# Heads of an mLSTM mixer on one Trainium2 core: row selection by matmul against rows read back by DMA, chunk 0 without its state product, output transposes in another PSUM bank

## What is computed

```python
b = jnp.swapaxes(jnp.cumsum(lfb, axis=1), 1, 2)
inter = b + m[..., None]
Dm = jnp.where(causal, b[..., :, None] - b[..., None, :] + ih[..., None, :], -jnp.inf)
m_t = jnp.maximum(inter, jnp.max(Dm, axis=-1))
w_inter = jnp.exp(inter - m_t)
s = jnp.einsum('blhd,bshd->bhls', qb, kb) * jnp.exp(Dm - m_t[..., None])
num = w_inter[..., None] * jnp.einsum('blhd,bhde->bhle', qb, C) + jnp.einsum('bhls,bshe->bhle', s, vb)
den = w_inter * jnp.einsum('blhd,bhd->bhl', qb, n) + jnp.sum(s, axis=-1)
h = num / jnp.maximum(jnp.abs(den), jnp.exp(-m_t))[..., None]
C_new = a_prev[..., None, None] * C + jnp.einsum('bshd,bshe->bhde', kw, vb)
```

## Time and profile before

| | us |
|---|---|
| median of 3 runs | 2975.05 |
| lowest and highest run | 2974.89, 2980.57 |
| profiled execution, its own time | 2982.64 |
| its span in the trace | 2980.9 |
| PE busy (matmuls) | 2853.4 |
| DVE busy | 1445.9 |
| ACT busy | 861.9 |
| POOL busy | 130.8 |

### The profile page before, as it was taken

How to read it: one execution, slowest core, us unless ns; L and a number is a source line. 1 busy time by engine, 2 the same in 40 slices (tenths; PEclk the granted TensorE clock), 3 DMA queues, 4 the chain that set the end, 5 groups by cost and what they waited for, 6 DMA issues and landing times. The chain is left out here.

```text
span 2980.9 us, 44355 instructions
## 1 busy us (share of the span) xinstructions
PE 2853.4 (96%) x17489; PEld 2738.9 (92%) x17489; DVE 1445.9 (49%) x3014; ACT 861.9 (29%) x1392; POOL 130.8 (4%) x190
## 2 busy tenths in 40 slices
PE   5899999999999898999999999999899999999997
PEld 3799999999999888989989988998799999999996
DVE  4655454455443736246436434634773434444346
ACT  5422222222213422332333233234531111111114
POOL 2100000000003000000000000000200000000002
PEclk7899999999999999999999999999999999999998
DMA  7133223222210114111111211212111111111111
GB/s 231 45 97 99 98 84 98 98 84 89 66 52 7 57 42 126 50 57 55 53 61 39 66 57 50 69 54 64 54 43 43 42 42 42 42 42 42 42 43 60
DMA packets 167523, 192.98 MB, mean 65 GB/s; under 512 B 7760, under 2 KB 157036, under 8 KB 167349
## 3 DMA queue, kind: packets, MB, share of 16 engines
q1 hardware_dynamic: 166962, 191.12, 20.1%
q10 hardware_dynamic: 342, 0.15, 0.0%
q0 software_dynamic: 96, 0.00, 0.0%
HBM read 172.38 MB, written 18.87 MB: 64 GB/s over the span
## 5 line engine op out<-in xcount | busy, mean ns | idle before, releaser
L521 DVE SCALAR_TENSOR_TENSOR xT<-ps,gate_p,xT 128x384 f32<-128x384 f32 (+1 forms) x624 | 347.3, 571 | 110.5 <-PE ps L801 97.4
L907 PE MATMUL ps<-hhi,mw_hi 128*128 128x384 f32 (+1 forms) x1152 | 387.8, 337 | 9.6 <-DVE mw_lo L1690 7.6
L738 DVE TENSOR_TENSOR hf<-st,ps 128x384 f32<-128x384 f32 x132 | 70.2, 532 | 642.6 <-PE ps L822 640.5
L908 PE MATMUL ps<-hlo,mw_hi 128*128 128x384 f32 (+1 forms) x1152 | 379.4, 329 | 0.0
L909 PE MATMUL ps<-hhi,mw_lo 128*128 128x384 f32 (+1 forms) x1152 | 379.0, 329 | 0.0
L820 PE MATMUL ps<-hhi,wa_hi 128*128 128x384 f32 (+1 forms) x1056 | 349.9, 331 | 16.9 <-DVE wa_lo L728 13.9
L821 PE MATMUL ps<-hlo,wa_hi 128*128 128x384 f32 (+1 forms) x1056 | 347.5, 329 | 0.0
L822 PE MATMUL ps<-hhi,wa_lo 128*128 128x384 f32 (+1 forms) x1056 | 347.1, 329 | 0.0
L820 PE MATMUL ps<-hhi,wb_hi 128*128 128x384 f32 (+1 forms) x1056 | 346.2, 328 | 0.3 <-DVE wb_lo L728 0.3
L822 PE MATMUL ps<-hhi,wb_lo 128*128 128x384 f32 (+1 forms) x1056 | 346.0, 328 | 0.0
L821 PE MATMUL ps<-hlo,wb_hi 128*128 128x384 f32 (+1 forms) x1056 | 345.9, 328 | 0.0
(11 more groups left out here) (295 smaller groups left out, 5141.2 us busy)
## 6 DMA issues: line engine op xcount, KB each, us to landing
ada_raw<-in_w_ada SPq DMA_DIRECT2D x36, 1024.0 KB, 5.1
mw_raw<-in_w_in SPq DMA_DIRECT2D x32, 1024.0 KB, 5.9
wa_raw<-in_w_ffn_in SPq DMA_DIRECT2D x22, 1024.0 KB, 5.1
wb_raw<-in_w_ffn_in SPq DMA_DIRECT2D x22, 1024.0 KB, 5.2
wo_raw<-in_w_ffn_out SPq DMA_DIRECT2D x22, 1024.0 KB, 5.0
ada_raw<-in_w_ada_final SPq DMA_DIRECT2D x8, 1024.0 KB, 5.4
cs<-in_state_mlstm_C SPq DMA_DIRECT2D x32, 256.0 KB, 2.7
out_C_sample<-cs SPq DMA_DIRECT2D x32, 256.0 KB, 2.2
```

The lines of the kernel that those rows point to most:

```text
L521: ins = dve.scalar_tensor_tensor(out=xT[:, m, t0:t0 + wp], in0=ps[:, bank, 0:wp], scalar=gate_p[:, m:m + 1], in1=xT[:, m, t0:t0 + wp], op0 ...
L738: dve.tensor_tensor(M["hf"][:, n, 0:w], M["st"][:, n, 0:w], ps[:, up_bank("b", b, i, n), 0:w], ALU.mult).then_inc(C["hidden"].sem, 1)
L907: pe.matmul(out, wh, xh, start=(j == 0), stop=False)
L908: pe.matmul(out, wh, xl, start=False, stop=False)
```

## The change

1. `m_rows` and `a_prev` are written to DRAM by SP in `gates_and_v` (two DMAs, `m_d` and `a_d`). SP reads row h of each back on all 128 partitions (`load_m`: `mb`, 128 x 1088 numbers, and `ap_`, 128 x 16), for head 0 when the block `heads` begins, for the others at the end of the head before, ahead of the store of the prompt state. `sel`, L1934, L2008 and L1848 go. DVE's subtraction reads `mb` in SBUF and no longer waits for the products of stage 0; that wait now stands behind it.
2. Chunk 0 has no state product (L1947, L1597 of that chunk go); DVE copies the score product and the state update from PSUM where it added before; `C` is no longer cleared.
3. The output transposes of stage 2 go to bank 3, columns 256 to 511. They wait for `st_done` of the job after in place of `inter_done`. Key transposes of job p wait for `inter_done` of job p-1, and keys times queries of job p for `h_kept` of job p-2.

The diff, cut:

```diff
@@ gates_and_v, SP
+                    sp.dma_start(m_d[:, :], m_rows[:, :]).then_inc(m_out.sem, 16)
...
+                    sp.wait_ge(*e_done(1))
+                    sp.dma_start(a_d[:, :], a_prev[:, :]).then_inc(m_out.sem, 16)
@@ heads, SP, end of a head, behind the wait for c_upd(h * 8 + 8)
+                        if not last:
+                            sp.wait_ge(*K["e_ready"](h * NJ + NJ))
+                            load_m(h + 1)
...
+                    def load_m(h):
+                        sp.dma_start(mb[:, :], m_d[bass.ds(h, 1), :].broadcast_to([P, T])).then_inc(K["mb_in"].sem, 16)
+                        sp.dma_start(ap_[:, :], a_d[bass.ds(h, 1), :].broadcast_to([P, 16])).then_inc(K["mb_in"].sem, 16)
@@ heads, ACT
-                        if chunk:
-                            act.wait_ge(*K["inter_mm"](h * 8 + c + 1))
+                        if chunk and c:
+                            act.wait_ge(*K["inter_mm"](h * 7 + c))
...
-                            ins = act.activation(q[:, i, t0:t0 + L], ps[:, 4, 128 * i:128 * i + L], ACT.Copy, scale=ng[:, i:i + 1])
+                            ins = act.activation(q[:, i, t0:t0 + L], ps[:, 3, 256 + 128 * i:256 + 128 * i + L], ACT.Copy, scale=ng[:, i:i + 1])
@@ heads, DVE
-                        dve.tensor_copy(sel[:, :], ident[0:H, bass.ds(h, 1)].broadcast_to([H, P])).then_inc(*own.one())
-                        dve.memset(C[:, :, :], 0.0).then_inc(*own.one())
...
-                        dve.wait_ge(*K["s0"](h * NJ + p + 1))
-                        dve.tensor_tensor(ex[0:L, 0:L], mask[:, :], ps[0:L, 3, 128:128 + L], ALU.subtract).then_inc(K["e_ready"].sem, 1)
+                        if p == 0:
+                            dve.wait_ge(*K["mb_in"](h * 32 + 32))
+                        dve.tensor_tensor(ex[0:L, 0:L], mask[:, :], mb[0:L, t0:t0 + L], ALU.subtract).then_inc(K["e_ready"].sem, 1)
                         if p:
                             scaled(h, p - 1)
-                        else:
+                        dve.wait_ge(*K["s0"](h * NJ + p + 1))
+                        if p == 0:
                             state_n(h)
...
-                        dve.tensor_copy(ap_[:, :], ps[:, 3, 0:16]).then_inc(K["ap_kept"].sem, 1)
@@ heads, PE, stage 0
                             elif p == 1:
-                                pe.wait_ge(*K["inter_done"](h * 8 + 1))
+                                pe.wait_ge(*K["kw_done"](h * NJ + 2))
                             else:
-                                pe.wait_ge(*K["h_kept"](h * NJ + p - 1))
+                                pe.wait_ge(*K["inter_done"](h * 7 + p - 1))
...
+                            if p >= 2:
+                                pe.wait_ge(*K["h_kept"](h * NJ + p - 1))
...
-                        ins = pe.matmul(ps[0:L, 3, 128:128 + L], sel[:, 0:L], M["m_rows"][:, t0:t0 + L], start=True, stop=True)
@@ heads, PE, stage 2
-                        if p < 7:
-                            pe.wait_ge(*K["inter_done"](h * 8 + p + 2))
-                        else:
-                            pe.wait_ge(*K["h_kept"](h * NJ + p))
+                        pe.wait_ge(*K["st_done"](h * NJ + min(p + 2, NJ)))
...
-                        pe.matmul(ps[:, 3, 0:16], sel[:, :], M["a_prev"][:, :], start=True, stop=True).then_inc(K["ap_mm"].sem, 1)
```

More of the change, by code:

```diff
@@ L40 @@
 EPS = 1e-6
-HEAD_STEPS = 148
+HEAD_STEPS = 146
 BIG = 1.0e30
@@ L912, in layer, with gates_and_v @@
         w_d = I["w_in"][0].rearrange("(k p) n -> p k n", p=P)
-        def gates_and_v(M, v_at, free, v_raw, norm):
+        def gates_and_v(M, v_at, free, v_raw, norm, m_d, a_d):
             ar.at = free
@@ L1366, in spatial, with heads @@
             return [v_out(16)] + [mix_out[t](16 * (3 if t == 0 else 2)) for t in range(SLOTS)]
-        def heads(M, free, mixed_d, stored):
+        def heads(M, free, mixed_d, stored, m_d, a_d):
             ar.at = free
@@ L1520, in body @@
                             load(h + 1, 1)
+                    def load_m(h):
+                        sp.dma_start(mb[:, :], m_d[bass.ds(h, 1), :].broadcast_to([P, T])).then_inc(K["mb_in"].sem, 16)
+                        sp.dma_start(ap_[:, :], a_d[bass.ds(h, 1), :].broadcast_to([P, 16])).then_inc(K["mb_in"].sem, 16)
                     for done in stored:
                         sp.wait_ge(*done)
+                    load_m(0)
                     with sp.Fori(0, H - 1) as h:
@@ L1781, in stage1 @@
                         dve.wait_ge(*K["s1"](h * NJ + p + 1))
-                        if chunk:
-                            dve.wait_ge(*K["inter_done"](h * 8 + c + 1))
+                        if chunk and c:
+                            dve.wait_ge(*K["inter_done"](h * 7 + c))
                         if p:
@@ L1786, in stage1 @@
                         src = inter if chunk else inter_s
-                        ins = dve.tensor_tensor(num[0:L, :], src[0:L, :], ps[0:L, 5, 0:DH + 1], ALU.add)
+                        if p:
+                            ins = dve.tensor_tensor(num[0:L, :], src[0:L, :], ps[0:L, 5, 0:DH + 1], ALU.add)
+                        else:
+                            ins = dve.tensor_copy(num[0:L, :], ps[0:L, 5, 0:DH + 1])
                         ins.then_inc(K["b5_read"].sem, 1)
@@ L1798, in stage1 @@
                                           ).then_inc(K["var_ready"].sem, 1)
-                        if chunk:
+                        if chunk and c == 0:
+                            dve.tensor_copy(C[:, :, :], ps[:, 6:8, 0:DH + 1]).then_inc(K["c_upd"].sem, 1)
+                        elif chunk:
                             dve.scalar_tensor_tensor(out=C[:, :, :], in0=C[:, :, :], scalar=ap_[:, c:c + 1],
@@ L1932, in stage0 @@
                         for i in range(2):
-                            pe.matmul(ps[0:L, 3, 0:L], kk[:, i, t0:t0 + L], q[:, i, t0:t0 + L], start=(i == 0), stop=(i == 1))
-                        ins = pe.matmul(ps[0:L, 3, 128:128 + L], sel[:, 0:L], M["m_rows"][:, t0:t0 + L], start=True, stop=True)
+                            ins = pe.matmul(ps[0:L, 3, 0:L], kk[:, i, t0:t0 + L], q[:, i, t0:t0 + L], start=(i == 0), stop=(i == 1))
                         if p == 0:
@@ L1943, in stage1 @@
                             pe.wait_ge(*K["kw_done"](h * NJ + c + 2))
-                            if c:
-                                pe.wait_ge(*K["c_upd"](h * 8 + c))
+                        if chunk and c:
+                            pe.wait_ge(*K["c_upd"](h * 8 + c))
                             for i in range(2):
@@ L2131, in layer @@
         mixed_d = nc.dram_tensor("mixed", [D, T], F32, kind="Internal").ap()
+        m_d = nc.dram_tensor("m_rows_out", [H, T], F32, kind="Internal").ap()
+        a_d = nc.dram_tensor("a_prev_rows", [H, 16], F32, kind="Internal").ap()
         head_w_in = [cnt("h_w_in0"), cnt("h_w_in1")]
-        S = gates_and_v(M, after, ar.at, v, Norm(V_MIX, 24, 32, gate=40, factor=1.0))
+        S = gates_and_v(M, after, ar.at, v, Norm(V_MIX, 24, 32, gate=40, factor=1.0), m_d, a_d)
         stored = spatial(M, S, after + NTT * D * 4, v, mixed_d)
-        heads(M, after, mixed_d, stored)
+        heads(M, after, mixed_d, stored, m_d, a_d)
         ffn(I["w_ffn2_in"][0], I["w_ffn2_out"][0], Norm(V_FFN2, 48, 56, gate=64, factor=0.5))
```

16 lines of the change are left out of this document (6 added, 10 removed).

## The result

| | median | runs | ratio, 95% interval |
|---|---|---|---|
| before | 2974.97 us | 2974.28 to 2980.57 | |
| after | 2945.16 us | 2943.91 to 2947.61 | 0.9897 [0.988, 0.9914] |
| after, second time | 2946.22 us | 2943.99 to 2949.89 | 0.9896 [0.9877, 0.9916] |

Before stands here with a fourth run beside the three of the forecast. The change takes 29.8 us off, and 30.1 the second time (2976.34 less 2946.22); 27.9 were forecast, and both times lie in the range.

The account below looks back on a forecast made before the run. The prediction took PE's own matmul stream in the heads as the bound. Its terms, 14.2 + 1.3 + 3.5 + 8.9 = 27.9 us, came off the median 2975.05, giving 2947.1 us; range 2937 to 2957.

Parts of the forecast that it names:

- Term 1: PE's selecting matmuls in the stages (9 jobs by 4 heads): removing them takes 14.2 us off, lower end 9.2.
- The neighbour's price: Rival at the selecting matmuls: each worth its neighbour's 0.27 us, so 9.2 us off there, 2952.2 in all; chance 0.04.
- Term 2: PE's selection of `a_prev`, once a head: removing it takes 1.3 us off, and PE's next wait stays.
- Term 3: Chunk 0's state product on PE: removing it takes 3.5 us off, 0.87 in each of 4 heads.
- Term 4: PE's wait at the output transposes for ACT's read of `inter`: 8.9 us off, ends 0 and 8.9.
- The new wait for term 4: Rival: PE waits at the sample product or key transposes instead, all of Term 4 given back, 2956.0 us; chance 0.10.
- The clock: Rival, PE's clock at stage entry: three falls end, 2937.5 us, chance 0.11; or one comes per head, 2959.9, chance 0.05.
- The slow rival: End of heads 0 to 2: broadcast reads delay the store of `C` by 30 us, time 2981 us; chance 0.02.

Follow-up runs that it names:

- before again: The kernel before, run once more without edits: 2976.95 us, ratio 0.9999 to its other runs.
- selections back: The changed kernel with PE's two selecting products put back, their results not used: 2965.44 us.
- bank 3 alone: The kernel before with only the output transposes moved to bank 3 and their waits changed: 2965.59 us, ratio 0.9956.

## Why the prediction was right

Right: the sign, the bound (PE's own stream in the heads) and every term's place. The sum of 27.9 came within 1.9 and 2.2 us of the 29.8 and 30.1, in part by luck: one term was 3.0 too small, and 1.2 that was not foreseen went back.

- **Term 1, 14.2.** Right: the step is 0.41 us with the selection back. The neighbour's price (9.2) fell: the product over 4 rows took 0.41 us here, its neighbour over 128 took 0.27. The changeover between unlike products is not the whole of it: in the trace of before the selection's two instructions start at 1250.14 and 1250.35, 0.21 apart, and its neighbour's with as many columns 0.11 apart (1249.60, 1249.71). The rule that I weighed, of the Trainium skill (TensorE: Matmul & The Clock Gate, "Why this matters for your kernels"), says of 32 rows that they take the time of 128; for 4 rows these steps do not agree with it.
- **Term 2, 1.3.** The 0.32 us are right; that PE's next wait "has nothing to do with it and stays" was wrong. Entry into the stages after, timeline, head 0:

```profile
1216.56 0.38 PE L2020 MATMUL ps<-ident,kk 128*64 128x128 f32 x2
...
1217.16 0.47 ACT L1651 ACTIVATE kws<-ps,tk 64x256 f32<-64x256 f32 x1
...
1217.78 0.41 PE L1938 MATMUL ps<-ident,kk 128*128 128x128 f32 x2 [0.84 <-ACT kws L1651]
```

  `kws` starts 0.60 us behind the transposes, with no idle time of ACT ahead of it; before, ACT had waited for these transposes and PE stood 0.65. PE now comes earlier than ACT is free, and 0.19 a head, 0.8 us, goes back.
- **Term 3, 3.5.** Right: 0.86 a head when put back.
- **Term 4, 8.9: mis-sized; it measured 11.9 us.** I took the idle time that the rows show. Around the wait in the earlier trace rows, the state update of before starts at 1308.67 and the transposes at 1310.88, 2.21 us; after, 0.87 for the same step, 1303.90 to 1304.77. The line of before:

```profile
1308.67 1.03 PE L1958 MATMUL ps<-vx,kw 128*128 128x257 f32 x4
```

  The wait cost 1.34 and shows as 1.17, because the idle time is counted from the end of the last matmul (1.03 us long), and without a wait the next one starts 0.16 before that end. Over 15 waits this makes 11.3 us, and 0.6 more lies in the step behind each, which was 0.17 to 0.21 and is 0.14.
- **The new wait for term 4.** The place was right (the sample product, for DVE's update of `C`). The margin of 0.1 us became a wait of 0.14, because PE gained 0.17 more at the wait than I had counted and 0.05 in the step behind it; it gives back 0.4 us in all, not 8.9.
- **The clock.** The likeliest case was that it stays out of the median, and the medians agree: 29.9 without any fall. Yet in the profiles the falls at the entry did go: 7 of 16 heads of the four profiles with the selections (before three, before again one, selections back one, bank 3 alone two), and none of 36 in the nine without. Were they as frequent in the unprofiled runs, the gain would have been nearer 35. Both profiled executions of before are among the eight slowest of the 47 (2982.64 and 2981.33), so falls may be rarer in the others; no profile shows it, and it stays open.
- **The slow rival.** Not met: 18.8 us of margin, as read. With the queue held the loss was far smaller than priced, and the path that shows is the next head's weights behind the store, not DVE's late start.

The sum as measured: 14.2 + 1.3 + 3.5 + 11.9 - 0.8 - 0.4 = 29.7.

## What to carry to other kernels

Price a stall on PE by start-to-start times, with the wait and without it at the same step, not by the idle time in its row, and look for waits too short to be listed. Where a stall goes, follow the next condition to a tenth of a microsecond and multiply what is short by the number of places: it turns a fear of losing the whole term into 0.4 us. A short product costs what its own step shows, from its start to the next start. A DMA held up in a queue delays all that stands behind it, here the next weights. Work brought forward on DVE is in somebody's way: see which of its results PE awaits there.

## What the runs showed of the hardware

A product over 4 rows took 0.41 us, longer than one over 128 rows with the same columns, 0.27; its two instructions stand 0.21 us apart, those of the other 0.11. With 0.73 us of small products more in the thin stretch at the entry, the clock fell to its lower level in some heads and not in others of one execution (0.87 against 1.00 mean for the same instructions, 25.88 against 22.86 us); without them it fell at the entry in no profile. Eight awaited broadcasts of one row of 4352 bytes to 128 partitions took the queue 34.9 us in head 0 (1356.11 to 1391.01), 4.4 each, with a median of 3.7 from issue to landing; the single ones of after took 5.9.
